# The second half of the adaLN modulation product: VectorE weighing replaced by TensorE products with the vector c

## The chip, the cores and the metric
The kernel runs on one core of one Trainium2 chip, as one launch. The metric is device time in microseconds, median of repeated executions; one further execution was profiled.

## What is computed
Two transformer-like blocks of two layers each run one after the other on 512 tokens of width 1024. Only a piece of the first block matters here: each of its layers derives six vectors of 1024 from the conditioning vector c and scales and shifts its two norms and gates its two residuals with them.

```python
c_act = jax.nn.silu(c)
for l in range(DEPTH):                                    # DEPTH = 2, D = 1024
    mod = (c_act @ ada_w[l] + ada_b[l])[:, None, :]       # ada_w[l]: 1024 x 6144, 24 MB
    sh1, sc1, g1, sh2, sc2, g2 = jnp.split(mod, 6, axis=-1)
    h = rmsnorm(x, norm_mix_g[l]) * (1.0 + sc1) + sh1
    ...                                                   # four mixers -> mix
    x = x + g1 * (mix @ w_out[l])                         # the output projection
    h = rmsnorm(x, norm_ffn_g[l]) * (1.0 + sc2) + sh2     # needs columns 3072.. of mod
    f = (silu(h @ ffn_w1[l]) * (h @ ffn_w3[l])) @ ffn_w2[l]
    x = x + g2 * f
```

## The kernel before
All large products are made in three TensorE products each (`three`, lines 1967 to 1969): weights and activations are both split into a high and a low part. ScalarE makes the high part of a weight block (L781), GpSimd the low one (L1236), and TensorE multiplies them with 512 tokens as the moving operand. A unit (`pe_unit`) is 256 output columns of a weight matrix with 1024 rows: two tiles m = 0, 1, each of 8 rows blocks k times three matmuls, into PSUM banks 0 and 1, so 48 matmuls in a unit. Weights come in units through two buffers `raw[0]`, `raw[1]`, all DMAs being issued by SyncE (SP) in program order.

The modulation matrix of a layer is cut into chunks of 256 columns (`G`). Chunks 0 to 15 (the first 4096 columns) are made elsewhere and belong to `a_raw` and `a_acc`. The last eight, `B_CHUNKS = 8`, are the ones this change touches; they are made during the output projection of the same layer:
- SP (`sp_modulation_b`, L607 to L614) loads chunk n into `b_raw[n % 2]`, a tile of 128 partitions x 8 row blocks x 256 columns. From the third chunk on it waits until chunk n - 2 has been weighed. In `sp_layer1` chunks 0 and 1 go ahead of weight unit 12, chunks 2 and 3 ahead of unit 13, and chunks 4 to 7 behind unit 13 and ahead of the first FFN weights.
- VectorE (`weigh_b`, L1674, by `dve_weigh`, L1424) multiplies row block 0 by c (L1428) and adds the seven others, each times its own c (L1431), into `b_acc`: eight instructions of 128 x 256 for each chunk. Each waits for the one before. Two chunks stand ahead of the projection's residual updates, the others are placed between them: in the loop over the eight tiles k, for k from 1 to 6, chunk k + 1 is weighed first, and then tile k of the projection is taken out of its bank (L1684, `x = bank * g1 + x`), which also frees the bank for TensorE. Sums of squares for the next norm (L1468) follow from tile 2 on.
- TensorE sums `b_acc` over its 128 partitions with a moving operand of one column, a column of ones (L2245), two output columns of bank 6 for a chunk. After each of the four projection units (`pe_layer1`, the loop over j) it does so for two chunks. The last of them lets VectorE add the bias and make the gains (L1449, L1458), which the norm ahead of the FFN needs.

After the last of these TensorE makes the sum over partitions for the norm (`pe_rms`, L2034), ScalarE takes its inverse root (L796, L798), VectorE multiplies (L1485), ScalarE makes the normed high part (L802) and the full one, VectorE the low one (L1481), and the FFN starts with the first pair of units (`pe_first_pair`). ScalarE splits FFN unit 14 ahead of its square of tile 6 and unit 15 after its square of tile 7. In this span the order on every engine is that of the program text; no scheduler moves anything.

Of the kernel before, what the change touches and what calls it, by code (L numbers as in the profile page):

```python
# [20 lines left out]
F32 = mybir.dt.float32  # L21
# [6 lines left out]
P = 128  # L28
T = 512
D = 1024  # L30
KD = D // P
NB = T // P
G = 256
# [15 lines left out]
A_CHUNKS, B_CHUNKS = 16, 8  # L49
# [61 lines left out]
def build(nc, a, table_at, out):  # L111

    with ExitStack() as ctx:
        top = [nc.sbuf_base + 31 & ~31]

        def place(name, shape, dt, at=None):

            size = 4
            for x in shape[1:]:
                size *= x  # L120
            off = top[0] if at is None else at
            t = nc.alloc_sbuf_tensor_at(name, shape, dt, offset=off)
            if at is None:
                top[0] = off + (size + 31 & ~31)
            return t

        b = Named()
# [75 lines left out]
        m = Region("m_", mid)  # L203
# [14 lines left out]
        fq_at = m.at  # L218
# [16 lines left out]
        b.rows2 = place("rows2", [2 * TAPS, P], F32, at=(nc.sbuf_usable_end & ~31) - 4 * P)  # L235

        b.b_raw = [place(f"b_raw{i}", [P, KD, G], F32, at=full_at + 4 * KD * G * i) for i in range(2)]
        b.b_acc = place("b_acc", [P, B_CHUNKS * G], F32, at=fq_at)

        n = Region("n_", mid)  # L240
        b.n_sq = n("sq", [P, KD, T])
# [43 lines left out]
        bank = [ctx.enter_context(nc.psum_tensor(f"bank{i}", [P, T], F32)) for i in range(8)]  # L285
        s = Sems(nc, ctx)
# [35 lines left out]
class Sems:  # L322

    def __init__(self, nc, ctx):
        def up(name, per, credit=0):

            return Signal(ctx.enter_context(nc.semaphore(name)), per, credit)
# [16 lines left out]
        self.par = up("par", 2)  # L344
        self.a_acc = up("a_acc", KD * A_CHUNKS, 2 * KD)
        self.a_pe = up("a_pe", 2)
        self.b_acc = up("b_acc", KD * B_CHUNKS)
        self.b_pe = up("b_pe", 1)
        self.mod = up("mod", 3)
        self.gain = up("gain", 2)  # L350
        self.a_in = [up(f"a_in{i}", 16 * A_CHUNKS // 2) for i in range(4)]
# [255 lines left out]
def sp_modulation_b(sp, e, l, n):  # L607

    s = e.s
    if n >= 2:  # L610
        sp.wait_ge(*s.b_acc(l, KD * (n - 1)))
    c = (A_CHUNKS + n) * G
    sp.dma_start(e.b.b_raw[n % 2][:, :, :], e.a["ada_w"][l, :, c:c + G].rearrange("(k p) c -> p k c", p=P))\
      .then_inc(s.b_in[n % 2].up, 16)  # L614
# [35 lines left out]
def sp_layer1(sp, e, l, more):  # L650
    a, b, s = e.a, e.b, e.s
    lay = Layer(s, 1, l)

    for j in range(2):
        sp_weights(sp, e, lay, j, a["w_in"], l, IN1[UNIT_COLS1[j]])
    sp.wait_ge(*lay.bank_free(0, 0))
    sp.wait_ge(*lay.bank_free(1, 0))
    sp.wait_ge(*s.r(l * 2, 1))
    sp.dma_start(b.decay[:, :, :], a["decay"]).then_inc(s.decay_in.up, 16)
    for m in range(2):  # L660
        sp.dma_start(b.pw[:, m, :], a["pool_w"][l, 2 * m:2 * m + 2, :, :].rearrange("e c d -> (e c) d"))\
          .then_inc(s.decay_in.up, 16)
    for j in range(2, 10):
        sp_weights(sp, e, lay, j, a["w_in"], l, IN1[UNIT_COLS1[j]])
    for j in range(4):
        if j == 2:
            sp.wait_ge(*s.gn_o(l, 2))
        if j >= 2:
            for n in (2 * j - 4, 2 * j - 3):
                sp_modulation_b(sp, e, l, n)  # L670
        sp_weights(sp, e, lay, 10 + j, a["w_out"], l, G * j)
    for n in range(4, B_CHUNKS):
        sp_modulation_b(sp, e, l, n)
    sp_ffn(sp, e, lay, 14, a["ffn_w1"], a["ffn_w3"], 0, a["ffn_w2"], l, more)
    if more:
        sp_parameters(sp, e, l + 1)
# [747 lines left out]
def dve_weigh(dve, raw, acc, c, up, base, ks=range(KD)):  # L1424

    for k in ks:
        if k == 0:
            dve.tensor_scalar(acc, raw[:, 0, :], c[:, 0:1], None, ALU.mult).then_inc(up, 1)  # L1428
        else:
            dve.wait_ge(up, base + k)  # L1430
            dve.scalar_tensor_tensor(acc, raw[:, k - ks[0], :], c[:, k:k + 1], acc, ALU.mult, ALU.add)\  # L1431
               .then_inc(up, 1)
# [20 lines left out]
def dve_gains(dve, e, l, norm):  # L1453

    s, b = e.s, e.b
    dve_mod(dve, e, l, 2 * norm)
    dve.wait_ge(*s.mod(l, 2 * norm + 1))
    dve.scalar_tensor_tensor(b.gain[:, 8 * norm:8 * norm + 8], b.mod[:, 8 + 24 * norm:16 + 24 * norm], 1.0,  # L1458
                             b.par[:, 8 * norm:8 * norm + 8], ALU.add, ALU.mult).then_inc(s.gain.up, 1)


def dve_rms_sum(dve, e, c, k, total, square):

    s = e.s
    dve.wait_ge(*s.sq(c, k + 1))
    if k > 1:
        dve.wait_ge(*s.ssq(c, k - 1))
    dve.tensor_tensor(total, total, square, ALU.add).then_inc(s.ssq.up, 1)  # L1468
# [66 lines left out]
def dve_layer1(dve, e, l, more):  # L1535
    s, b, bank = e.s, e.b, e.bank
# [134 lines left out]
    for m in range(2):  # L1671
        dve.tensor_tensor(b.ln_d[:, m, :], b.ln_d[:, m, :], b.r[:, :], ALU.mult).then_inc(s.cn_xr.up, 1)

    def weigh_b(n):  # L1674
        dve.wait_ge(*s.b_in[n % 2](l, 16 * (n // 2) + 16))
        dve_weigh(dve, b.b_raw[n % 2], b.b_acc[:, n * G:(n + 1) * G], b.c, *s.b_acc(l, KD * n))

    weigh_b(0)
    weigh_b(1)
    for k in range(KD):  # L1680
        if k >= 1 and k + 1 < B_CHUNKS:
            weigh_b(k + 1)
        dve.wait_ge(*s.tile(lay.pair(5 + k // 4), k // 2 % 2, k % 2))
        dve.scalar_tensor_tensor(b.x[:, k, :], bank[k % 2][:, :], b.mod[:, 16 + k:17 + k], b.x[:, k, :],  # L1684
                                 ALU.mult, ALU.add).then_inc(s.bank[k % 2].up, 1)
        if k >= 2:
            dve_rms_sum(dve, e, l * 2 + 1, k - 1, b.sq[:, 0, :], b.sq[:, k - 1, :])
    dve_rms_sum(dve, e, l * 2 + 1, KD - 1, b.sq[:, 0, :], b.sq[:, KD - 1, :])
    dve.wait_ge(*s.b_pe(l, 1))
    dve_gains(dve, e, l, 1)  # L1690
    dve_rms(dve, e, l * 2 + 1, b.hf, s.hl)
    dve_ffn(dve, e, lay, 14, (Q_FFN,))
# [236 lines left out]
def dve_program(dve, e):  # L1929
    s, b, bank = e.s, e.b, e.bank  # L1930
    for x in (s.bank0, s.bank1, s.up0, s.up1, s.a_acc, s.lx):
        dve.sem_inc(x.up, x.credit)
    dve_setup(dve, e)

    dve.wait_ge(s.z_x.up, KD + 2)
    with dve.Fori(0, A_CHUNKS // 4) as i:
        for p in range(2):
            dve_modulation(dve, e, 0, i, p)
    dve.wait_ge(s.z_copied.up, Z_COPIES)
    dve.wait_ge(s.trig_in.up, 16)  # L1940
    dve_trig(dve, e, 0)
    with dve.Fori(A_CHUNKS // 4, A_CHUNKS // 2) as i:
        for p in range(2):
            dve_modulation(dve, e, 0, i, p)
    for l in range(DEPTH):
        dve_layer1(dve, e, l, l < DEPTH - 1)
    dve_rms(dve, e, 2 * DEPTH, b.x, s.lhl)
    dve.wait_ge(s.trig_in.up, 32)
    dve_trig(dve, e, 1)
    for l in range(DEPTH):  # L1950
        dve_layer2(dve, e, l)
    dve_output(dve, e)
# [19 lines left out]
def pe_unit(pe, e, lay, j, q, order=range(KD), ready=None, banks=None, tokens=False):  # L1972

    pe_unit_at(pe, e, lay, j // 2, j % 2, q, order, ready, banks, tokens)
# [56 lines left out]
def pe_rms(pe, e, c, total):  # L2031
    s, b = e.s, e.b
    pe.wait_ge(*s.ssq(c, 7))
    pe.matmul(e.bank[7][:, :], b.ones[:, :], total, start=True, stop=True).then_inc(s.rms.up, 1)  # L2034
# [65 lines left out]
def pe_layer1(pe, e, l):  # L2100
    s, b, bank = e.s, e.b, e.bank
# [82 lines left out]
    for k in range(KD):  # L2184
        pe.wait_ge(*s.hf(c, k + 1))
        op = pe.matmul(bank[4][0:4, :], b.wff[:, k, :], b.hf[:, k, :], start=(k == 0), stop=(k == KD - 1))
# [31 lines left out]
    for m in range(2):  # L2218
        lone_wait(pe, s, *lay.bank_free(m, Q_POOL))
        for h in range(2):  # L2220
            o = HD * h
            op = pe.matmul(bank[m][o:o + HD, :], b.pw[o:o + HD, m, :], b.wb[o:o + HD, m, 0:T], start=True, stop=True)
# [6 lines left out]
    for m in range(2):  # L2229
        op = pe.matmul(bank[0][:, :], b.ones[:, :], b.cv[:, m, :], start=(m == 0), stop=(m == 1))  # L2230
# [3 lines left out]
    for m in range(2):  # L2234
        pe.wait_ge(*s.cn_sq(l, m + 1))
        op = pe.matmul(bank[1][:, :], b.ones[:, :], b.ln_s[:, m, :], start=(m == 0), stop=(m == 1))
    op.then_inc(s.cn_ps.up, 1)
    values(3)
    for j in range(4):
        pe_unit(pe, e, lay, 10 + j, Q_OUT + j, order=MIX_ORDER, ready=(lambda n: s.ml(l, n + 1)) if j == 0 else None)  # L2240

        pe.wait_ge(*s.b_acc(l, KD * (2 * j + 2)))
        for n in range(4 * j, 4 * j + 4):
            at = 2 * A_CHUNKS + n
            op = pe.matmul(bank[6][:, at:at + 1], b.b_acc[:, n * P:(n + 1) * P], b.ones[:, 0:1], start=True, stop=True)  # L2245
    op.then_inc(s.b_pe.up, 1)
    pe_rms(pe, e, c + 1, b.sq[:, 0, :])
    pe_ffn(pe, e, lay, 14, c + 1)

# [313 lines left out]
```

## Time and profile before

| | |
|---|---|
| median of 3 runs | 2858.13 us (2850.03 to 2858.3) |
| profiled execution | 2860.76 us, of which the span is 2858.9 us |
| mean granted TensorE clock in the span | 0.937 of full speed |
| TensorE matmul busy | 2610.1 us, 91% |
| VectorE busy | 1081.4 us, 38% |
| ScalarE busy | 876.8 us, 31% |
| GpSimd busy | 1109.1 us, 39% |
| DMA, mean | 94 GB/s |

A share of busy time is an average over the whole span. The change concerns two stretches of it, one in each layer of the first block, some 69 us long each; so the page's averages say who bounds the kernel as a whole, and a timeline of these stretches says who bounds there. A matmul's duration in the timeline holds its way through the array and overlaps the next one's: the cost of one in a row of many is the distance from start to start.

### The profile page before, as it was taken

The numbers are of one execution on the slowest core, as the hardware profiler recorded it, in microseconds if no ns is written. First come the engines' busy times: TensorE is split into PE (matmuls) and PEld (weight loads), VectorE is DVE, ScalarE is ACT, GpSimd is POOL, SyncE is SP. The second block draws the span as 40 slices with busy tenths as digits, with TensorE's granted clock in tenths as the row PEclk, the third lists the DMA queues.
The fourth block names the chain that finished last, engine by engine and source line by source line (L and its number), as shares of the span: only waits on it lengthen the run. The fifth ranks groups of instructions, "written<-read, shape, count | busy, mean of one in ns | idle before, by whom it ended". The sixth has DMA issues, their size and how long they took to land.

```text
span 2858.9 us, 30619 instructions
## 1 busy us (share of the span) xinstructions
PE 2610.1 (91%) x11550; PEld 2040.0 (71%) x11550; DVE 1081.4 (38%) x1830; ACT 876.8 (31%) x1158; POOL 1109.1 (39%) x376
## 2 busy tenths in 40 slices
PE   1599789999999779999899989999989898999998
PEld 1485568878876468887677668887868566888786
DVE  7575640018756560000159543000025954300002
ACT  1323342222323342222142452222133245322212
POOL 0232235544333225554334224555432422555441
PEclk6699889999899889999999899999999889999998
DMA  7420333247521333322232022332342111232231
GB/s 234 137 82 24 125 111 103 88 121 224 171 74 45 104 105 101 103 89 81 80 91 74 23 74 80 97 103 76 89 112 59 60 37 59 88 103 89 84 91 60
DMA packets 313580, 267.98 MB, mean 94 GB/s; under 512 B 20376, under 2 KB 306696, under 8 KB 313240
## 3 DMA queue, kind: packets, MB, share of 16 engines
q1 hardware_dynamic: 313496, 266.86, 30.1%
q8 instruction: 52, 0.85, 0.1%
q14 instruction: 32, 0.26, 0.0%
HBM read 264.74 MB, written 2.10 MB: 93 GB/s over the span
## 4 chain that ended last, share of the span: by engine, by line
PE 79%; DVE 9%; issue 6%; ACT 3%; POOL 2%; DMA 1%; DVEq 0%; SPq 0%; ACTq 0%; POOLq 0%
PE bank L1967 23%; PE bank L1969 23%; PE bank L1968 23%; DVE a_acc L1431 2%; PE bank L2257 1%; POOL w_lo L1236 1%; PE bank L2059 1%; DVE m_sq L1468 1%; DVE n_work L1809 1%; DVE n_top L1805 1%; PE bank L2170 1%; PE bank L2322 1%; PE bank L2139 1%; PE bank L2109 1%; ACT w_hi L781 1%
## 5 line engine op out<-in xcount | busy, mean ns | idle before, releaser
L1236 POOL TENSOR_TENSOR w_lo<-raw,w_hi 128x2048 fp32r<-128x2048 f32 (+1 forms) x216 | 912.1, 4223 | 1254.2 <-ACT w_hi L781 1223.4
L1967 PE MATMUL bank<-h_hi,w_lo 128*128 128x512 f32 (+1 forms) x2256 | 898.5, 398 | 52.9 <-DVE h_lo L1481 18.2
L1968 PE MATMUL bank<-h_lo,w_hi 128*128 128x512 f32 (+1 forms) x2256 | 888.3, 394 | 0.0
L1969 PE MATMUL bank<-h_hi,w_hi 128*128 128x512 f32 (+1 forms) x2256 | 887.0, 393 | 0.0
L1967 PEld LDWEIGHTS bank<-h_hi,w_lo 128*128 128x128 f32 (+1 forms) x2256 | 429.2, 190 | 166.1 <-issue 52.4
L781 ACT ACTIVATE w_hi<-raw 128x2048 fp32r<-128x2048 f32 (+1 forms) x216 | 378.0, 1750 | 505.7 <-PE bank L1969 443.5
L1968 PEld LDWEIGHTS bank<-h_lo,w_hi 128*128 128x128 f32 (+1 forms) x2256 | 429.5, 190 | 91.5 <-issue 2.4
L1969 PEld LDWEIGHTS bank<-h_hi,w_hi 128*128 128x128 f32 (+1 forms) x2256 | 429.1, 190 | 92.1 <-issue 0.4
L1528 DVE TENSOR_TENSOR f_full<-f_act,bank 128x512 f32<-128x512 f32 x88 | 60.5, 687 | 884.2 <-PE bank L1969 884.2
L1967 PE MATMUL bank<-f_hi,w_lo 128*128 128x512 f32 x704 | 280.8, 399 | 13.3 <-POOL f_lo L1248 13.3
L1969 PE MATMUL bank<-f_hi,w_hi 128*128 128x512 f32 x704 | 280.5, 398 | 0.0
L1968 PE MATMUL bank<-f_lo,w_hi 128*128 128x512 f32 x704 | 279.9, 398 | 0.0
L1248 POOL TENSOR_TENSOR f_lo<-f_full,f_hi 128x512 f32 (+1 forms) x88 | 113.9, 1295 | 185.3 <-ACT f_hi L824 185.3
L824 ACT ACTIVATE f_hi<-f_full 128x512 f32 (+1 forms) x88 | 55.6, 632 | 377.7 <-DVE f_full L1528 377.7
L1967 PEld LDWEIGHTS bank<-f_hi,w_lo 128*128 128x128 f32 x704 | 134.2, 191 | 46.4 <-issue 14.9
L1968 PEld LDWEIGHTS bank<-f_lo,w_hi 128*128 128x128 f32 x704 | 134.4, 191 | 31.3
L1969 PEld LDWEIGHTS bank<-f_hi,w_hi 128*128 128x128 f32 x704 | 133.9, 190 | 31.5
L1431 DVE SCALAR_TENSOR_TENSOR a_acc<-a_raw,c,a_acc 128x256 f32 (+1 forms) x224 | 146.0, 652 | 9.5 <-DMA a_raw<-in_ada_w 0.4
L818 ACT ACTIVATE f_act<-bank 128x512 f32<-128x512 f32 x88 | 52.9, 601 | 307.7 <-PE bank L1969 307.7
L1924 DVE TENSOR_TENSOR x<-bank,x 128x512 f32<-128x512 f32 x16 | 11.1, 692 | 235.7 <-PE bank L1969 235.7
L1580 DVE SCALAR_TENSOR_TENSOR m_cv<-m_ch,taps,m_cv 128x512 f32<-128x512 f32 x120 | 95.5, 865 | 0.1
L1967 PE MATMUL bank<-w_hi,h_lo 128*128 128x256 f32 (+1 forms) x320 | 90.8, 284 | 0.0
(290 smaller groups left out, 2403.7 us busy)
## 6 DMA issues: line engine op xcount, KB each, us to landing
raw<-in_ffn_w SPq DMA_DIRECT2D x44, 1024.0 KB
raw<-in_w_ffn_in SPq DMA_DIRECT2D x44, 1024.0 KB
raw<-in_w_in SPq DMA_DIRECT2D x34, 1024.0 KB
a_raw<-in_ada_w SPq DMA_DIRECT2D x64, 512.0 KB, 4.8
raw<-in_ffn_w SPq DMA_DIRECT2D x32, 704.0 KB
raw<-in_w_ffn_out SPq DMA_DIRECT2D x32, 704.0 KB
b_raw<-in_ada_w SPq DMA_DIRECT2D x16, 1024.0 KB, 5.0
raw<-in_w_out SPq DMA_DIRECT2D x8, 1024.0 KB
```

The source lines that it names most:

```text
L781: act.activation(b.w_hi[p][:, 0:n], b.raw[p][:, 0:n], ACT.Copy).then_inc(s.hi.up, 1)
L818: act.activation(b.f_act[:, m, :], bank[m][:, :], ACT.Silu).then_inc(s.bank[m].up, 1)
L824: act.activation(cols(b.f_hi, i * 2 + m), b.f_full[:, m, :], ACT.Copy).then_inc(s.fh.up, 1)
L1236: pool.tensor_tensor(b.w_lo[p][:, 0:n], b.raw[p][:, 0:n], b.w_hi[p][:, 0:n].bitcast(F32), ALU.subtract)\
L1248: pool.tensor_tensor(cols(b.f_lo, i * 2 + m), b.f_full[:, m, :], cols(b.f_hi, i * 2 + m).bitcast(F32), ALU.subtract).then_inc(s.fl.up, 1)
L1431: dve.scalar_tensor_tensor(acc, raw[:, k - ks[0], :], c[:, k:k + 1], acc, ALU.mult, ALU.add)\
L1468: dve.tensor_tensor(total, total, square, ALU.add).then_inc(s.ssq.up, 1)
L1528: dve.tensor_tensor(b.f_full[:, m, :], b.f_act[:, m, :], bank[2 + m][:, :], ALU.mult)\
L1580: dve.scalar_tensor_tensor(b.cv[:, m, :], b.ch[:, m, t:t + T], b.taps[:, n:n + 1], b.cv[:, m, :], ALU.mult, ALU.add).then_inc(s.conv.up, 1)
L1967: pe.matmul(out, wlo, xhi, start=start, stop=False)
L1968: pe.matmul(out, whi, xlo, start=False, stop=False)
L1969: return pe.matmul(out, whi, xhi, start=False, stop=stop)
```

## The change
VectorE no longer weighs the last eight chunks, and `b_acc` is gone. TensorE multiplies the raw chunk by c itself: the 128 x 128 block (k, m) of `b_raw` is the stationary operand, column k of `c` the moving one, and eight such products accumulate in one column of bank 6. A chunk takes 2 x 8 of them instead of two. They stand where the sums over partitions stood, two chunks after each of the four units. The semaphore `b_acc` goes too: SP now waits for TensorE to have finished chunk n - 2 before it loads chunk n, and TensorE waits for a chunk's DMA.

```diff
 def sp_modulation_b(sp, e, l, n):
     if n >= 2:
-        sp.wait_ge(*s.b_acc(l, KD * (n - 1)))
+        sp.wait_ge(*s.b_pe(l, n - 1))
...
-    def weigh_b(n):
-        dve.wait_ge(*s.b_in[n % 2](l, 16 * (n // 2) + 16))
-        dve_weigh(dve, b.b_raw[n % 2], b.b_acc[:, n * G:(n + 1) * G], b.c, *s.b_acc(l, KD * n))
-
-    weigh_b(0)
-    weigh_b(1)
     for k in range(KD):
-        if k >= 1 and k + 1 < B_CHUNKS:
-            weigh_b(k + 1)
...
-    dve.wait_ge(*s.b_pe(l, 1))
+    dve.wait_ge(*s.b_pe(l, B_CHUNKS))
...
     for j in range(4):
         pe_unit(pe, e, lay, 10 + j, Q_OUT + j, ...)
-        pe.wait_ge(*s.b_acc(l, KD * (2 * j + 2)))
-        for n in range(4 * j, 4 * j + 4):
-            at = 2 * A_CHUNKS + n
-            op = pe.matmul(bank[6][:, at:at + 1], b.b_acc[:, n * P:(n + 1) * P], b.ones[:, 0:1], start=True, stop=True)
-    op.then_inc(s.b_pe.up, 1)
+        for n in (2 * j, 2 * j + 1):
+            pe.wait_ge(*s.b_in[n % 2](l, 16 * (n // 2) + 16))
+            for m in range(2):
+                at = 2 * (A_CHUNKS + n) + m
+                for k in range(KD):
+                    op = pe.matmul(bank[6][:, at:at + 1], b.b_raw[n % 2][:, k, m * P:(m + 1) * P], b.c[:, k:k + 1],
+                                   start=(k == 0), stop=(k == KD - 1))
+            op.then_inc(s.b_pe.up, 1)
```

## Rows read from the trace of the kernel before
**Rows 1.** The page, chain that ended last: shares of the span by engine.
```profile
PE 79%; DVE 9%; issue 6%; ACT 3%; POOL 2%; DMA 1%; DVEq 0%; SPq 0%; ACTq 0%; POOLq 0%
```
**Rows 2.** Groups of instructions by line and form: count | busy us, mean ns | idle before.
```profile
L1431 DVE SCALAR_TENSOR_TENSOR b_acc<-b_raw,c,b_acc 128x256 f32<-128x256 f32 x112 | 68.4, 611 | 4.0
L2245 PE MATMUL bank<-ones,b_acc 128*128 128x1 f32 x64 | 7.6, 240 | 0.0
```
**Rows 3.** Windows over both layers: length, busy us (count) by engine, clock, DMA.
```profile
316.50:385.50 69.00, 52.90 (x228) 41.46 (x226) 54.20 (x85) 22.13 (x26) 22.68 (x7) 0.89 0.49 159
975.30:1044.30 69.00, 52.88 (x227) 41.48 (x226) 57.88 (x85) 22.25 (x26) 22.54 (x7) 0.89 0.49 158
```
**Rows 4.** Timeline of TensorE, layer 0: start us, us, engine, line, operation, [idle before].
```profile
331.13 0.95 PE L2245 MATMUL bank<-ones,b_acc 128*128 128x1 f32 x8
331.95 0.47 PE L1967 MATMUL bank<-h_hi,w_lo 128*128 128x512 f32 x1
...
342.96 0.95 PE L2245 MATMUL bank<-ones,b_acc 128*128 128x1 f32 x8
...
355.00 0.79 PE L1967 MATMUL bank<-h_hi,w_lo 128*128 128x512 f32 x1 [5.50 <-DVE x L1684]
...
376.94 2.08 PE L2034 MATMUL bank<-m_sq,ones 128*128 128x512 f32 x2 [1.45 <-DVE m_sq L1468]
385.57 0.76 PE L1967 MATMUL bank<-h_hi,w_lo 128*128 128x512 f32 x1 [6.56 <-DVE h_lo L1481]
```
**Rows 5.** Timeline of VectorE in the same stretch.
```profile
346.21 4.17 DVE L1468 TENSOR_TENSOR m_sq<-m_sq 128x512 f32<-128x512 f32 x1 [5.19 <-ACT m_sq L789]
...
350.68 3.61 DVE L1431 SCALAR_TENSOR_TENSOR b_acc<-b_raw,c,b_acc 128x256 f32<-128x256 f32 x7
354.20 0.74 DVE L1684 SCALAR_TENSOR_TENSOR x<-bank,mod,x 128x512 f32<-128x512 f32 x1
...
374.74 0.75 DVE L1684 SCALAR_TENSOR_TENSOR x<-bank,mod,x 128x512 f32<-128x512 f32 x1 [3.69 <-PE bank L1969]
...
380.43 3.85 DVE L1485 TENSOR_TENSOR m_sq<-x,r 128x512 f32<-128x512 f32 x3 [3.27 <-ACT r L798]
```
**Rows 6.** Timeline of TensorE at other places: long batches of one-column products.
```profile
52.94 6.96 PE L2109 MATMUL bank<-ones,a_acc 128*128 128x1 f32 x32 [33.50 <-DVE a_acc L1431]
...
104.74 6.83 PE L2109 MATMUL bank<-ones,a_acc 128*128 128x1 f32 x32
...
756.51 4.57 PE L2109 MATMUL bank<-ones,a_acc 128*128 128x1 f32 x32
```
**Rows 7.** Windows over the last of these batches, L2109 on TensorE alone: length, busy (count), clock, DMA.
```profile
757.50:758.50 1.00, 1.00 (x11) 1.00 0.00 0
759.00:760.00 1.00, 1.00 (x7) 0.50 0.00 0
```
**Rows 8.** Timeline of TensorE after the batch at 104.74.
```profile
111.43 0.77 PE L1967 MATMUL bank<-h_hi,w_lo 128*128 128x512 f32 x1
112.00 0.63 PE L1968 MATMUL bank<-h_lo,w_hi 128*128 128x512 f32 x1
...
117.12 0.46 PE L1968 MATMUL bank<-h_lo,w_hi 128*128 128x512 f32 x1
```
**Rows 9.** Windows, all engines, layer 0: columns as in rows 3.
```profile
355.00:360.00 5.00, 5.00 (x13) 3.94 (x14) 4.75 (x10) 0.61 (x1) 0.00 (x0) 0.54 0.64 210
...
389.00:391.00 2.00, 2.00 (x7) 1.56 (x7) 1.89 (x4) 2.00 (x4) 0.00 (x0) 0.67 0.00 0
```
**Rows 10.** Timeline of the DMA queue, ScalarE and GpSimd, layer 0.
```profile
331.26 28.59 SPq L613 DMA_DIRECT2D b_raw<-in_ada_w  x4
360.28 58.15 SPq L587 DMA_DIRECT2D raw<-in_ffn_w  x6
...
368.65 1.92 ACT L781 ACTIVATE w_hi<-raw 128x2048 fp32r<-128x2048 f32 x1 [2.70 <-DMA raw<-in_ffn_w]
...
378.03 4.50 POOL L1236 TENSOR_TENSOR w_lo<-raw,w_hi 128x2048 fp32r<-128x2048 f32 x1 [2.53 <-ACT w_hi L781]
```

More of the change, by code:

```diff
@@ L237, in build @@
         b.b_raw = [place(f"b_raw{i}", [P, KD, G], F32, at=full_at + 4 * KD * G * i) for i in range(2)]
-        b.b_acc = place("b_acc", [P, B_CHUNKS * G], F32, at=fq_at)
         n = Region("n_", mid)
@@ L346, in __init__ @@
         self.a_pe = up("a_pe", 2)
-        self.b_acc = up("b_acc", KD * B_CHUNKS)
-        self.b_pe = up("b_pe", 1)
+        self.b_pe = up("b_pe", B_CHUNKS)
         self.mod = up("mod", 3)
```

## The prediction, on record before the changed kernel was run
> **What bounds the kernel now.** I read the page's chain first: TensorE holds 79% of it, VectorE 9% [rows 1]. So TensorE's own time counts nearly everywhere, and VectorE only where TensorE waits for it. Then the groups: VectorE's weighing of the last eight chunks is 68.4 us (and 5.5 us for the first row blocks), TensorE's part of the same work 7.6 us [rows 2]. On the page's averages TensorE, busy for 91%, is the wrong engine to give work to and VectorE, at 38%, the wrong one to relieve; but the stretch decides. In the two stretches concerned VectorE is busy for 54.20 and 57.88 of 69 us and TensorE for 52.9 [rows 3]: here they are rivals, and the weighing is three quarters of VectorE's time. The two layers look alike, so I work out one and double it.
>
> The stretch that changes runs from the end of the first projection unit (331.13) to the first FFN matmul (385.57): 54.44 us [rows 4]. Three units of 48 matmuls take 11.0 us each where nothing stops them (331.95 to 342.96), so 33.0 us. The rest is 21.4 us: four batches of eight one-column records, 0.82 us from their start to the next unit's (331.13 to 331.95), 3.3 us; a stall of 5.50 us at 355.00, with a slow restart; 1.45 us ahead of the norm's sum; and 8.63 us from that sum (376.94) to the FFN [rows 4]. The stall is the weighing's: a sum of squares of 4.17 us, seven weighing steps of 3.61 us and only then the residual update at 354.20 that frees the bank [rows 5]. It also costs clock: with TensorE idle the granted clock fell to 1.2 GHz, and over 355 to 360 it averages 0.54 [rows 9].
>
> **What goes.** Eight chunks of weighing a layer, 37 us of VectorE. Of it only the stall was on TensorE's path: 5.5 us, and with it the half-speed restart (about 4.6 us at 0.43 instead of 0.23 us a matmul, some 2.1 us lost). The 4 x 0.82 us go as well, since the new batches replace them. Nothing else is late next: the residual update behind tile 3 still waits for the slow sum of squares ahead of it, but in the meantime TensorE has a batch of at least 7 us to do. The other sum of squares, mod and gains follow the last tile by about 2 us, under the last batch.
>
> **What comes.** 8 chunks x 2 halves x 8 row blocks = 128 products in a layer, 32 in a batch. The trace has 64 matmul records of L2245 for 32 products of the program [rows 2]: an fp32 product is two load-and-multiply pairs. So a batch is 64 pairs. The price of a pair is that of L2109, the same shape, a 128 x 128 fp32 block against one column: 32 pairs took 6.96 and 6.83 us, 0.214 us a pair, at 1.2 GHz [rows 6], and 11 pairs in each 1 us but the edges, 0.111 us a pair, at 2.4 GHz [rows 7]. The latter is what a batch costs if the clock stays up: 64 x 0.1115 = 7.1 us. The two passes of one product already add into the same column there, so I add nothing for adding up.
>
> **The clock decides between these prices.** The batch at 756.51 began behind dense work at 2.4 GHz, ran without a gap, and yet the clock fell within it, 2.0 to 2.5 us after its start; the window from 759 holds 7 records at 0.50 [rows 6, 7]. And the batches at 52.94 and 104.74, nearly 7 us each of back-to-back pairs, stayed at half speed from end to end [rows 6]. 512-column matmuls behind the latter began at 111.43 and ran 0.427 us apart (12 steps from 112.00 to 117.12), until the clock rose 5.7 us after their start [rows 8]. So one-column products, however tightly packed, neither hold the clock nor bring it back. The present batches of 0.82 us are too short to show it. The Trainium skill, "TensorE: Matmul & The Clock Gate", section "Loop structure matters more than you think", promises that back-to-back matmuls stay warm; taken at its word the batches would cost 7.1 us each. The trace disagrees (0.214 us a pair behind a fall to 0.50), and that rule is the first rival below.
>
> How far into a batch it falls is not tied to the batch's start: 2.0 to 2.5 us in the only case. For the stall it is about 3 us (TensorE idle from 349.5, windows at 0.54 behind it), and between rise and fall the chip takes its own moments: rises come 5.7 us after dense work starts [rows 8], about 4.5 us behind 355.00 and behind 385.57 [rows 4, 9]. I take 3.5 us (bounds 2 and 5). A batch is then 3.5 + (64 - 31.4) x 0.2137 = 10.5 us (bounds 11.8 and 9.1). A unit behind it starts at half speed for 5 us (4.5 to 5.7), losing 5 x (1 - 0.2275 / 0.4267) = 2.3 us: 13.3 us (13.1 to 13.7).
>
> **Queues and waits.** SP now waits for TensorE before chunks 2 to 7, with weight unit 13 behind chunk 3 and the FFN weights behind chunk 7. Chunk 7's load waits for chunk 5, the end of the third batch, then the first FFN weights go out. They took 368.65 - 360.28 = 8.4 us to land, 1.9 us on ScalarE, and some 4.6 us on GpSimd [rows 10]; the second copy waits on ScalarE for the square of the last tile. That puts the second low part some 8 us behind the last unit's end, while the FFN can't start for over 17 us after it. A chunk is asked for when the one two before it is done, so a unit (11 us) and half a batch or more before its own turn, above the 8.4 us of that row. All hidden; if the cover went, the second copy would cost what it is late. One gain: VectorE's three multiplications at 380.43 took 3.85 us where the usual one takes 0.68; the first waited for GpSimd's second copy (378.03 + 4.50) [rows 5, 10]. After, that copy is done in time: 1.8 us less, 8.63 - 1.8 = 6.8 us from the norm's sum to the FFN. The last batch stands ahead of the norm's sum on TensorE, so it is exposed in full.
>
> **The sum for a layer**, from 331.13: four batches 4 x 10.5 = 41.9; three units 3 x 13.3 = 39.9; the tail 6.8; together 88.6 us against 54.4: +34 us. Bounds: late falls and early rises, 4 x 9.1 + 3 x 13.1 + 6.8 = 82.5, +28.1; the reverse, and the tail as it is, 4 x 11.8 + 3 x 13.7 + 8.6 = 96.9, +42.5. Two layers: +68 us (56 to 85). The profiled execution would go from 2860.76 to 2929; it lies 2.6 us above the median, so the median of 2858.13 goes to **2926 us**.
>
> **Rivals.**
> 1. The clock holds through the batches (weight loads count as work for the gate). Batches 7.1, units 11.0: 28.5 + 33.0 + 6.8 = 68.3, +13.9 a layer, 2886 us. For it: the engine never idles. Against: rows 6 and 7. 0.07.
> 2. It gets faster. Freed are 21.4 - 6.8 = 14.6 us a layer, so it is faster if the four batches together cost less than that, 256 pairs at under 0.057 us, with the clock up. The place would be the load of the next block hiding entirely under the product before it, or one pass instead of two: 128 pairs x 0.1115 = 14.3 us, 0.3 us a layer better, 2857.5 us; with both, 128 x 0.057 = 7.3 us, 7.3 us a layer better, 2843.5 us. For it: nothing but VectorE's being the crowded engine here. Against: two records for each product, 0.1115 us for each. Faster 0.02; within 0.3%, by one of the two, 0.02.
> 3. The 16 passes into one PSUM column do not overlap: each waits out the product before, 0.24 us by the record's mean duration [rows 2] instead of the distance. Batches 15.4 at either clock: 61.4 + 39.9 + 6.8 = 108.1, +53.7 a layer, 2965 us. For it: sixteen in a row aren't in the trace, only two. Against: pairs of one product and of two products lie equally far apart. 0.06.
> 4. The change does less than it says (the batches wait for data, the queue of SP binds): every wait that I found is covered by 5 us or more; a wait of 5 us in one batch would give 10 us more, and lies inside the range. Not kept apart.
>
> **Chances.** Forecast 0.83, the rivals 0.07, 0.04, 0.06. 0.3% of 2858 is 8.6 us, about what a measurement of this kernel can tell from no change. Slower holds the forecast and rivals 1 and 3: 0.96. The range is the forecast's own bounds, 2914 to 2943, widened on the low side towards rival 1 and slightly above for a wait: 2906 to 2945.
>
> **What would show it.** No VectorE instruction of L1428 or L1431 between the projection's residual updates, and no stall of TensorE for L1684. Four batches of 64 matmul records between the units, 9 to 12 us each, about 0.11 us apart at first and 0.21 later; the clock down within each batch and up 4 to 6 us into the next unit; the FFN's first matmul some 88 us behind the first batch's start; the mean clock of the span down from 0.937 to about 0.926 (some 35 us a layer more at half speed: (2859 x 0.937 + 68 - 35) / 2927). The forecast is wrong if the batches keep 2.4 GHz (+28 us remain), if pairs in an accumulating row lie further apart than 0.214 us, or if the first FFN matmul waits for GpSimd's copy.

## The result

The changed kernel takes 2916.16 us in the median (2914.71 to 2919.93), the kernel before 2855.6 us beside it. The ratio is 1.0212, with a 95% interval of 1.0196 to 1.0227: 2.1% slower, some 60 us. The forecast was 2926 us, +68, within 2906 to 2945. The profiled execution took 2917.59 us, its span is 2915.8.

The page of the changed kernel: VectorE is relieved by 78 us, TensorE busy for 73 us more, and the new products have a line of their own in the chain (L2237 in the last line). The second line answers to [rows 1]: TensorE 81% instead of 79%, VectorE 8% instead of 9%.

```profile
PE 2683.5 (92%) x11998; PEld 2113.7 (72%) x11998; DVE 1003.2 (34%) x1702; ACT 876.7 (30%) x1158; POOL 1108.1 (38%) x376
...
PE 81%; DVE 8%; issue 6%; ACT 3%; POOL 2%; DMA 1%; DVEq 0%; SPq 0%; ACTq 0%; POOLq 0%
PE bank L1957 23%; PE bank L1958 23%; PE bank L1959 23%; PE bank L2237 2%; DVE a_acc L1429 2%; PE bank L2250 1%; POOL w_lo L1234 1%; PE bank L2049 1%; DVE n_work L1799 1%; DVE n_top L1795 1%; PE bank L2160 1%; PE bank L2315 1%; PE bank L2129 1%; PE bank L2099 1%; PE bank L2348 0%
```

Its groups by form hold 512 records for the 256 products, two each; this answers to [rows 2].

```profile
L2237 PE MATMUL bank<-c,b_raw 128*128 128x1 f32 x512 | 78.6, 290 | 0.0
```

The timeline of TensorE in layer 0, the answer to [rows 4]. Each line of L2237 is one batch of 64 pairs, the next line the first matmul of the unit behind it.

```profile
329.38 9.65 PE L2237 MATMUL bank<-c,b_raw 128*128 128x1 f32 x64
338.89 0.77 PE L1957 MATMUL bank<-h_hi,w_lo 128*128 128x512 f32 x1
...
352.27 8.73 PE L2237 MATMUL bank<-c,b_raw 128*128 128x1 f32 x64
360.87 0.77 PE L1957 MATMUL bank<-h_hi,w_lo 128*128 128x512 f32 x1
...
373.58 9.49 PE L2237 MATMUL bank<-c,b_raw 128*128 128x1 f32 x64
382.94 0.77 PE L1957 MATMUL bank<-h_hi,w_lo 128*128 128x512 f32 x1
...
396.48 11.69 PE L2237 MATMUL bank<-c,b_raw 128*128 128x1 f32 x64
408.04 2.06 PE L2024 MATMUL bank<-m_sq,ones 128*128 128x512 f32 x2
414.70 0.77 PE L1957 MATMUL bank<-h_hi,w_lo 128*128 128x512 f32 x1 [4.61 <-DVE h_lo L1479]
```

From the first batch to the FFN it takes 414.70 - 329.38 = 85.3 us where it took 54.4. From start to start the batches take 9.5, 8.6, 9.4 and 11.6 us, the units between them 13.4, 12.7 and 13.5, the tail 6.7. TensorE never waits between 329.38 and the end of the norm's sum: the 5.50 us stall of [rows 4] is gone. The windows tell where the length comes from (columns as in [rows 3]: the granted clock is the number behind the busy figures of the five engines):

```profile
329.40:338.90 9.50, 9.50 (x66) 9.50 (x64) 0.75 (x1) 1.91 (x1) 4.52 (x1) 0.73 0.34 110
338.90:343.90 5.00, 5.00 (x13) 3.94 (x14) 0.00 (x0) 0.00 (x0) 0.00 (x0) 0.50 0.75 244
344.00:352.00 8.00, 8.00 (x36) 6.63 (x36) 0.75 (x1) 0.00 (x0) 0.00 (x0) 1.00 0.32 107
352.30:360.90 8.60, 8.60 (x66) 8.60 (x64) 5.33 (x3) 4.09 (x5) 4.52 (x1) 0.81 0.37 122
373.60:382.90 9.30, 9.30 (x65) 9.30 (x64) 1.35 (x2) 0.63 (x1) 0.00 (x0) 0.74 0.37 115
396.50:408.00 11.50, 11.50 (x65) 11.50 (x64) 2.37 (x3) 2.43 (x2) 5.82 (x2) 0.59 0.46 147
...
1018.40:1027.40 9.00, 9.00 (x66) 9.00 (x64) 0.75 (x1) 1.91 (x1) 4.52 (x1) 0.77 0.35 117
1041.30:1052.50 11.20, 11.20 (x65) 11.20 (x64) 5.33 (x3) 4.10 (x5) 4.52 (x1) 0.61 0.28 94
1065.80:1074.50 8.70, 8.70 (x65) 8.70 (x64) 1.35 (x2) 0.63 (x1) 0.00 (x0) 0.80 0.37 121
1087.10:1096.60 9.50, 9.50 (x66) 9.50 (x64) 3.26 (x3) 2.43 (x2) 6.74 (x2) 0.73 0.39 117
```

All eight batches begin at 2.4 GHz and end at 1.2. Since the clock is at one of these two levels, a mean of 0.73 over 9.5 us means (0.73 - 0.5) / 0.5 = 46% of it at the upper one, 4.4 us; in the order of the lines 4.4, 5.3, 4.5, 2.1, 4.9, 2.5, 5.2 and 4.4 us, 4.2 in the mean. The unit behind starts at 0.50 (second line, 13 matmuls in 5 us) and is at 1.00 from 344 on (36 in 8 us).

The stretch from the first batch to the FFN grows by 30.9 us in layer 0 and by 30.4 in layer 1 (989.87 to 1044.33 before, 1018.36 to 1103.25 now), 61.3 us together. The FFN starts 29.1 us later in layer 0 (385.57 to 414.70), 58.9 us later in layer 1 (1044.33 to 1103.25), and the span ends 56.9 us later, so the rest of the kernel is 4 us shorter in this execution than in the one before.

### The profile page after: what moved, and what is told of

Same layout as the page of the kernel before. It is cut to its first block, busy times and chain, and to the rows that moved or that the text cites. A ratio compares the mean times of both kernels' runs of the same rounds, so it can differ in the third digit from the quotient of the medians.

```text
span 2915.8 us, 31387 instructions
## 1 busy us (share of the span) xinstructions
PE 2683.5 (92%) x11998; PEld 2113.7 (72%) x11998; DVE 1003.2 (34%) x1702; ACT 876.7 (30%) x1158; POOL 1108.1 (38%) x376
## 4 chain that ended last, share of the span: by engine, by line
PE 81%; DVE 8%; issue 6%; ACT 3%; POOL 2%; DMA 1%; DVEq 0%; SPq 0%; ACTq 0%; POOLq 0%
PE bank L1957 23%; PE bank L1958 23%; PE bank L1959 23%; PE bank L2237 2%; DVE a_acc L1429 2%; PE bank L2250 1%; POOL w_lo L1234 1%; PE bank L2049 1%; DVE n_work L1799 1%; DVE n_top L1795 1%; PE bank L2160 1%; PE bank L2315 1%; PE bank L2129 1%; PE bank L2099 1%; PE bank L2348 0%
## 5 line engine op out<-in xcount | busy, mean ns | idle before, releaser
L1957 PE MATMUL bank<-f_hi,w_lo 128*128 128x512 f32 x704 | 280.8, 399 | 13.3 <-POOL f_lo L1246 13.3
```

The costliest lines, as they stand in the source:

```text
L1957: pe.matmul(out, wlo, xhi, start=start, stop=False)
```

## The experiments

All kernels ran beside the kernel before. The question: how much of the 60 us is the pairs themselves, how much the clock, and what relieving VectorE gave back.

**1. The relief alone.** Based on the changed kernel; seven of eight row blocks are left out (and `start` and `stop` are True for the one that stays), so that TensorE has as many small products as before:

```diff
-                for k in range(KD):
+                for k in range(1):
```

> The changed kernel with only row block 0 of each chunk multiplied: 4 products (8 pairs) a batch as before, 7 of 8 row blocks of the second half of the modulation are left out. It shows what the relief of VectorE is worth by itself. My theory: the 5.50 us stall ahead of unit 2 goes for the most part (some 1.5 us stays, since the bank of tile 3 still waits for a sum of squares that waits for ScalarE), its half-speed restart goes (2.1 us), GpSimd's second copy may still delay the norm: 6 to 9 us a layer less than before, 2840 to 2846 us. The difference to the changed kernel, about 75 us, is then what 4 x 56 further pairs a layer cost with the clock that they lose, not the relief. Rival: VectorE was never in the way, this kernel takes as long as before (within 3 us), and the 60 us are the whole price of the batches.

Measured: 2858.73 us, ratio 1.0000 (0.9988 to 1.0013). The rival's number came out. But most of the stall did go, as the theory said; the time was lost again at the end of the stretch, in a place whose price I had not worked out. TensorE, VectorE and GpSimd of this kernel in layer 0:

```profile
350.63 0.50 PE L1957 MATMUL bank<-h_hi,w_lo 128*128 128x512 f32 x1 [1.59 <-DVE x L1674]
...
368.03 0.95 PE L2237 MATMUL bank<-c,b_raw 128*128 128x1 f32 x8
379.76 2.08 PE L2024 MATMUL bank<-m_sq,ones 128*128 128x512 f32 x2 [10.77 <-DVE m_sq L1466]
...
370.22 9.48 DVE L1466 TENSOR_TENSOR m_sq<-m_sq 128x512 f32<-128x512 f32 x2 [1.23 <-ACT m_sq L787]
...
369.74 9.41 POOL L1234 TENSOR_TENSOR w_lo<-raw,w_hi 128x2048 fp32r<-128x2048 f32 x2 [20.38 <-ACT w_hi L779]
```

The stall ahead of tile 5 is 1.59 instead of 5.50 us, and the last small batch comes at 368.03 instead of 374.54. The norm's sum, though, waits 10.77 us instead of 1.45 [rows 4] (10.39 in layer 1). VectorE's last two sums of squares take 9.48 us, where two took 1.48 elsewhere, since GpSimd's two splits of the first FFN weights run beside them without a break. The Trainium skill, "SBUF — State Buffer", section "SBUF: two separate sides", says that a VectorE operation with two SBUF inputs and a GpSimd operation that reads SBUF take a shared port pair as an exclusive lock, so that the one that comes second waits. The trace agrees: the two sums end at 379.70, 0.55 us behind the second split's end (379.15), and the single one at 345.74 ends 0.55 us behind the split of 344.74, too (4.17 us instead of 0.68). The splits come that late because the weights land at 367.76 only (issued at 358.17, behind the chunks' DMAs), and ScalarE makes its square of tile 6 behind the high part of the first of them.

**2. The same with the FFN weights earlier.** On SP's queue, the first two FFN units go ahead of chunks 6 and 7:

```diff
-    for n in range(4, B_CHUNKS):
+    for n in (4, 5):
         sp_modulation_b(sp, e, l, n)
-    sp_ffn(sp, e, lay, 14, a["ffn_w1"], a["ffn_w3"], 0, a["ffn_w2"], l, more)
+    for p, w in enumerate((a["ffn_w1"], a["ffn_w3"])):
+        sp_unit(sp, e, lay, 7, p, w8(b.raw[p]), w[l, :, 0:G].rearrange("(k p) c -> p k c", p=P))
+    for n in (6, 7):
+        sp_modulation_b(sp, e, l, n)
+    sp_ffn(sp, e, lay, 14, a["ffn_w1"], a["ffn_w3"], 0, a["ffn_w2"], l, more, first=1)
```

`first=1` lets its loop over the FFN's unit pairs start at the second.

> e1_relief (7 of 8 row blocks of the second half of the modulation left out, VectorE relieved) with the same early FFN weights. Theory: relieving VectorE by itself gives 6 us a layer once the splits are out of the way: the norm's sum 2 us behind the last batch instead of 11, 2845 us against e1_relief's 2859. Rival: no gain in the end, as e1_relief.

Measured: 2844.8 us, ratio 0.9955 (0.9939 to 0.9971), as the theory had it. GpSimd's splits now lie at 358.59 and 370.40, the two last sums between them, and the norm's sum 1.45 us behind the batch:

```profile
367.78 1.48 DVE L1470 TENSOR_TENSOR m_sq<-m_sq 128x512 f32<-128x512 f32 x2
...
358.59 4.61 POOL L1238 TENSOR_TENSOR w_lo<-raw,w_hi 128x2048 fp32r<-128x2048 f32 x1 [10.37 <-ACT w_hi L783]
370.40 4.50 POOL L1238 TENSOR_TENSOR w_lo<-raw,w_hi 128x2048 fp32r<-128x2048 f32 x1 [7.21 <-ACT w_hi L783]
...
369.31 1.12 PE L2028 MATMUL bank<-m_sq,ones 128*128 128x512 f32 x2 [1.45 <-DVE m_sq L1470]
```

In the trace the stretch from the first batch to the FFN takes 48.4 and 48.8 us in the two layers, against 54.4 and 54.5. So taking the weighing off VectorE is worth 13 us in both layers together, if the splits are out of the way, and nothing if they aren't. The same early weights in the kernel before:

> The kernel before with only the early FFN weights, VectorE's order as it was. Theory: GpSimd's first split comes some 2 us earlier only (it stands behind the square of tile 5 on ScalarE), the second stays where it is behind the square of the last tile, the stall stays: same as before within 3 us, so that e5's gain is of both steps together. Rival: the late weights alone are what binds, 8 us less than before.

Measured: 2855.09 us, ratio 0.9984 (0.9968 to 0.9999): some 4 us, at the edge of what shows, where I had expected no more than 3. They are not in this stretch: in the trace it takes 54.9 us in each layer, 0.4 more than before, and the stall is 5.50 us as before. Early weights alone are not the 13 us; it takes both.

**3. The clock, by a wider moving operand.** Based on the changed kernel; c's column is read 128 times over by a stride of 0:

```diff
-   op = pe.matmul(bank[6][:, at:at + 1], b.b_raw[n % 2][:, k, m * P:(m + 1) * P], b.c[:, k:k + 1],
+   op = pe.matmul(bank[6][:, at:at + P], b.b_raw[n % 2][:, k, m * P:(m + 1) * P], b.c[:, k:k + 1].to_broadcast([P, P]),
```

> The changed kernel with the moving operand of each product widened from 1 to 128 columns (c's column repeated by a stride of 0; the columns behind the wanted one are overwritten or unused), the result is the same. More work on TensorE: 128 columns in fp32 should take a quarter of the 0.53 us that 512 take, 0.134 us a pair at 2.4 GHz instead of 0.111. Theory (the gate looks at what streams, not at whether instructions are packed): the clock holds in the batches, 8.6 us each, units 11.0, 4 x 8.6 + 3 x 11.0 + 6.8 = 74 us from the first batch to the FFN instead of 85.3: 11 us a layer faster than the changed kernel although it streams 128 times the columns, about 2894 us. Rival (the gate falls for another reason: fp32 passes, load-bound pairs, bank 6): it falls as now, batches 13 to 14 us, about 2948 us.

Measured: 2877.82 us, ratio 1.0068 (1.0050 to 1.0085). By the medians 38 us less than the changed kernel, with 128 times the columns. TensorE's timeline and, below it, a window over the whole stretch:

```profile
330.69 7.31 PE L2237 MATMUL bank<-c,b_raw 128*128 128x128 f32 x64
...
384.93 7.31 PE L2237 MATMUL bank<-c,b_raw 128*128 128x128 f32 x64
...
330.70:392.00 61.30, 61.30 (x401) 55.54 (x399) 17.65 (x14) 12.14 (x12) 16.78 (x4) 1.00 0.50 162
```

The clock stays at 2.4 GHz up to the end of the last batch, in both layers, and each batch ahead of a unit takes 7.06 us to the unit's first matmul. I had expected 8.6, but a pair costs at most 0.1115 us, as with one column. That the columns stream while the next block loads would explain it; no row here shows it.

This is the cleanest pair of kernels of the study: same instructions, same data read, same order, and only the moving operand differs. The stretch from the first batch to the FFN takes 69.3 and 69.4 us instead of 85.3 and 84.9, 31.4 us less. It still holds waits of 2.06 and 2.15 us for VectorE's last sums, which the slower batches had covered. With these taken out, the fallen clock costs some 36 us in the changed kernel.

Another candidate for the fall was the DMA of the next chunk, which starts in the middle of a batch. In seven of the eight batches it is running within the microsecond in which the clock falls; in the eighth there is none (windows of TensorE alone: clock, DMA share, GB/s). And in the kernel above the same loads run beside the batches at a clock of 1.00.

```profile
333.40:334.40 1.00, 1.00 (x8) 0.69 0.28 62
...
1043.30:1044.30 1.00, 1.00 (x9) 0.72 0.00 0
```

**4. The clock, by the place of the products.** Two products behind each of the 16 three-matmul steps of a unit (`between`, chunk 2j + m in the half m), instead of 32 behind the unit:

```diff
+                if between is not None and n < KD - 1:
+                    between(m, n)
         op.then_inc(s.half.up, 1)
+        if between is not None:
+            between(m, KD - 1)
...
-        for n in (2 * j, 2 * j + 1):
...
```

> The changed kernel's products, all of them, but two behind each of the 16 three-matmul steps of their own unit instead of 32 behind the unit. Same instructions, same count. Theory (half of the loss is the clock that falls in a stretch of one-column products): with dense work in between, the clock holds; a unit takes 11.0 + 7.1 = 18.1 us, unit 0 takes part of it in its waits for GpSimd, no batch stands behind the last unit: some 13 us a layer over before, about 2883 us, 33 us faster than the changed kernel; this is also what the pairs cost at 2.4 GHz alone. Rival (pairs cost what they cost wherever they are; the fall comes anyhow): as the changed kernel, 2916, or slower, since a clock that fell once could not rise within a diluted unit: up to 2990.

Measured: 2879.93 us, ratio 1.0090 (1.0060 to 1.0119), 36 us less than the changed kernel, against 33 expected. The units run at full clock with the one-column products among them (first window; 0.99 over 989 to 1064 in layer 1); four pairs and three 512-column matmuls take 1.14 us, so a pair takes 0.114 us. The windows ahead of the norm's sum and across it (columns as before):

```profile
316.50:389.50 73.00, 73.00 (x450) 64.48 (x447) 11.71 (x13) 15.96 (x18) 17.54 (x6) 1.00 0.42 137
389.50:400.50 11.00, 1.59 (x6) 0.71 (x6) 8.09 (x10) 6.39 (x8) 4.50 (x1) 0.70 0.30 95
```

The second window holds what this order gives up: with no batch behind the last unit the norm's sum waits 1.90 us, and the FFN comes 8.63 us behind it, as before the change, instead of 6.66. That is 3.9 us a layer which the changed kernel doesn't have; on the other side the products of the first unit fill some of its waits for GpSimd. So the 36 us are near the clock's part, but are not that part alone.

**5. Shorter batches.** Row blocks 0 to 3 only (`for k in range(4)`, the other half of the products is left out), 32 pairs a batch:

> The changed kernel with row blocks 0 to 3 of 8 only (half of the products of the second half of the modulation are left out): batches of 32 pairs, 3.6 us at 2.4 GHz. Theory: the clock falls when a batch is long enough, and a batch of 32 pairs is near that: it falls in some batches and not in others, so they are 3.6 us where it holds and 4.5 to 5.5 us with a slow unit behind them where it falls; the price is less than half of the full batches': 2858 + 10 to 25 us. Rival: the clock falls in every batch as it does with 64 pairs and the units behind start slow: 2858 + 30 us or more, half of the price and more.

Measured: 2867.98 us, ratio 1.0038 (1.0023 to 1.0053), +11 us for half of the pairs where all of them cost +60. In layer 0:

```profile
329.47 3.63 PE L2237 MATMUL bank<-c,b_raw 128*128 128x1 f32 x32
...
345.58 4.75 PE L2237 MATMUL bank<-c,b_raw 128*128 128x1 f32 x32
...
363.29 3.63 PE L2237 MATMUL bank<-c,b_raw 128*128 128x1 f32 x32
...
377.80 3.63 PE L2237 MATMUL bank<-c,b_raw 128*128 128x1 f32 x32
```

The clock fell within one of the eight batches (the second of layer 0; 4.61 us to the unit behind it, the others 3.49), and soon behind two others, within the unit (12.6 us instead of 11.0 for the units behind the first of layer 0 and the second of layer 1). By the medians twice the pairs cost five times as much; by the two stretches of the traces, 65.9 and 63.1 us here, 20 us in sum against 61, it is three times. Not all of that is the clock: the last batch here lies ahead of a wait for VectorE's sums (7.28 us left, 10.77 in e1_relief), which it only shortens.

**6. Clock and queue mended together.** Wide operand and early weights:

> e2_wide (128-column moving operand, right result) with the same early FFN weights. In e2_wide the last sums of squares took 8.45 us beside GpSimd's back-to-back splits and put the norm's sum 2.3 us behind the last batch. Theory: these 2.3 us go in each layer, about 2873 us, still 15 us over before: with clock and queue mended, the change costs what its pairs cost at 2.4 GHz less the relief. Rival: same as e2_wide, 2878.

Measured: 2880.45 us, ratio 1.0083 (1.0063 to 1.0104); no gain over e2_wide, the rival's number. The profile shows that the theory's step did happen: the norm's sum comes at the end of the last batch (391.74), and the stretch takes 67.0 us in both layers where e2_wide has 69.3 and 69.4. These 2.3 us a layer are too little beside what executions of these kernels differ by (2870 to 2889 for e2_wide, 2877 to 2884 here). For the sum it matters that this kernel and e6_relief_early differ only in the products: 1.0083 - 0.9955 = 0.0128 of 2858 us, 37 us for the pairs at full clock.

**7. The relief without TensorE.** Can VectorE keep the weighing and the stall still go? On the kernel before:

> The kernel before, with VectorE keeping the weighing, but in another order: chunks 0 and 1 are weighed ahead of the wait for ScalarE's inverse root of the convolution's norm (VectorE is idle there for 10.8 us), each tile's residual update goes ahead of the next chunk's weighing, and the first sum of squares is put behind tile 3. Nothing is added to TensorE. Theory: the 5.50 us stall was one of order, not of VectorE's load; it goes, with its 2.1 us of restart: 7 to 8 us a layer, about 2842 us, which is all that relieving VectorE could give, at no cost on TensorE. Rival: VectorE is really full in this stretch (54 of 69 us), the stall moves to another tile or to the norm's sum, and the time stays within 3 us of before.

Measured: 2861.75 us, ratio 1.0020 (1.0007 to 1.0033), slower by 4 to 6 us, a miss. As in e1_relief the stall shrinks and the stretch gives it back. In layer 0 it is the same meeting of splits and sums of squares (9.42 and 9.13 us, and the norm's sum waits 9.10). In layer 1 the split comes earlier and holds up the weighing of the last chunk instead, 7.78 us for seven steps that take 3.61 elsewhere, and TensorE's small sum waits 3.48 us for it. With the early weights:

> e4_order, with the DMAs of the first two FFN weight units put ahead of those of chunks 6 and 7 on SP's queue. In the trace of e4_order the stall of 5.50 us ahead of unit 2 is down to 1.3 us, but the norm's sum comes 9.4 us behind the last batch instead of 1.7: the FFN weights land at 368.6, their two splits on GpSimd run back to back (9.42 us) right when VectorE wants its last two sums of squares (9.13 us for two instead of 1.4). Theory: the relief is real and is given back there, since the first split comes too late and meets the end of the projection; with the weights loaded earlier the first split is over before the last tile, the norm's sum comes 2 to 3 us behind the last batch, the FFN some 4 us a layer earlier than before: about 2850 us, the first version below the kernel before. Rival: the end of the stretch is bound by something else (the second split, behind the square of the last tile): within 3 us of before.

Measured: 2854.76 us, ratio 0.9989 (0.9979 to 1.0000); 3 us instead of 8, no better than the early weights alone; the stretch takes 54.3 us in each layer. What remained were TensorE's small sums waiting for chunks that were weighed late (1.87, 0.94 and 2.49 us in layer 0). So the chunks were moved further ahead:

```diff
+    weigh_b(2)
+    weigh_b(3)
     for k in range(KD):
...
-        if k >= 1 and k + 1 < B_CHUNKS:
-            weigh_b(k + 1)
+        if k in (1, 2, 4, 5):
+            weigh_b({1: 4, 2: 5, 4: 6, 5: 7}[k])
```

(the residual update of tile k stands first, in place of the line of dots; chunks 0 and 1 stand ahead of the wait for the convolution's norm and the first sum of squares behind tile 3, as in the two kernels before it, and chunk 6's DMA between those of the two FFN units).

> VectorE keeps the weighing; chunks 0 to 3 are weighed ahead of the first residual update (0 and 1 in the wait for the convolution's norm, 2 and 3 while TensorE is in unit 0), 4 and 5 behind the updates of tiles 1 and 2, 6 and 7 behind those of tiles 4 and 5; the updates always go first; the first FFN weights go ahead of the DMAs of chunks 6 and 7. In e5's trace what is left in this stretch are waits of TensorE's small sums for chunks 2 and 3 (2.25 us behind unit 1), 4 and 5 (1.3 us) and 6 and 7 (2.9 us within unit 3). Theory: with the chunks earlier these go too, units run back to back from unit 0 to the norm's sum, 8 us a layer less than before: 2843 to 2847 us, as e6_relief_early, which left most of the weighing out. Then all that the change could gain is to be had without TensorE. Rival: GpSimd's splits and VectorE's weighing stand in each other's way wherever they are put (a weighing step beside a split took 4.4 us more), and the time is e5's, 2855.

Measured: 2841.86 us, ratio 0.9941 (0.9920 to 0.9963), 0.6% below the kernel before and the fastest that gives the whole result, with VectorE doing all of its work. TensorE in layer 0:

```profile
329.91 0.95 PE L2253 MATMUL bank<-ones,b_acc 128*128 128x1 f32 x8
341.74 0.95 PE L2253 MATMUL bank<-ones,b_acc 128*128 128x1 f32 x8
353.57 0.95 PE L2253 MATMUL bank<-ones,b_acc 128*128 128x1 f32 x8
366.14 1.05 PE L2253 MATMUL bank<-ones,b_acc 128*128 128x1 f32 x8 [0.59 <-DVE b_acc L1434]
370.06 2.08 PE L2042 MATMUL bank<-m_sq,ones 128*128 128x512 f32 x2 [2.86 <-DVE m_sq L1471]
378.69 0.76 PE L1975 MATMUL bank<-h_hi,w_lo 128*128 128x512 f32 x1 [6.56 <-DVE h_lo L1484]
```

The first three small sums are 11.8 us apart, the fourth comes after 12.6, with a wait of 0.59; 378.69 - 329.91 = 48.8 us instead of 54.4 (47.6 in layer 1).

## Why the prediction was right, and where it was not

**The sum.** By ratios to the kernel before: relief -0.0045 (e6_relief_early), pairs at full clock +0.0128 (e7_wide_early against it), fallen clock 1.0212 - 1.0083 = +0.0129; together +0.0212. In us of 2858: -13, +37, +37. The parts are steps from one measured kernel to the next and so add up by construction, but the traces give the same by themselves. The two stretches together take 108.9 us before, 97.2 in e6_relief_early, 134.0 in e7_wide_early and 170.2 in the changed kernel: -12, +37, +36. The clock's part was forecast at 2 x (13.4 us of batches + 6.9 us of units) = 41 us. The 37 us for the pairs are net: at 7.06 instead of 0.82 us the four batches add 25 us a layer, and some 6 of these lie in waits that e6_relief_early still has.

The steps, one by one:

- **Two pairs for each product, at 0.1115 and 0.214 us**: right. 512 records; e2_wide's batches show 64 pairs in 7.06 us. Rival 3, passes that don't overlap when they add up in one column, is refuted by that and by the changed kernel's batches, 8.6 to 11.6 us where it has 15.4.
- **The clock falls within each batch and rises only in the next unit**: right in eight of eight. Rival 1 is out: its 2886 us is its forecast of the kernel with a clock that holds, and the kernels in which it held, e2_wide and e3_spread, are 8 and 6 us from it. The Trainium skill, "TensorE: Matmul & The Clock Gate", section "Loop structure matters more than you think", promises that back-to-back matmuls stay warm; for these one-column products the trace disagrees, with a granted clock of 0.50 at the end of eight of eight batches.
- **How far into the batch**: mis-sized. I took 3.5 us, 4.2 were measured (2.1 to 5.3, as wide as my bounds of 2 to 5). Batches of 10.5 us were forecast, 9.7 measured in the mean of eight (77.5 us in sum). That is 83.8 - 77.5 = 6.3 us, nearly all of the 7 us by which the two stretches came out below the forecast (68.4 forecast, 61.3 measured). The only batch in the trace before fell 2.0 to 2.5 us after its start, and six of the eight here took 4.4 to 5.3.
- **Units behind a batch**: 13.3 us forecast, 13.2 measured in six.
- **The tail**: 6.8 us forecast, 6.66 measured. The three multiplications that had taken 3.85 us beside GpSimd's split [rows 5] take 1.90 us, since that split is over by then.
- **Layers**: 85.3 and 84.9 us from batch to FFN against 88.6 forecast and 54.4 before. In layer 0 the stretch also began 1.75 us earlier (329.38 instead of 331.13). 0.4 us of it is GpSimd's low parts, 3.75 instead of 4.11 us with no weighing beside them; the rest was there ahead of the changed stretch and I have no cause for it but the differences between executions. In e1_relief, which has the same VectorE program, it began 0.5 us earlier only.
- **"Nothing else is late next"**: right for this kernel, wrong as a price of the relief. In the changed kernel the last sums of squares take 1.80 us and are over at 399.15, long before the last batch ends at 408.04, so it hides them. e1_relief and e4_order show that without such a batch the splits are late next, by 9.3 us (10.77 against 1.45) and, in layer 0, by 7.7 us (9.10); both of their forecasts failed on the step that carried this sentence over to them. The sum came out well here because the new work covered the spot: in this place the prediction was lucky.
- **Waits and queues**: all covered, as said. SP's FFN weights go out at 383.91, and GpSimd's second split ends at 399.98 + 4.51 = 404.5, 10 us ahead of the FFN. Rival 4 never came.
- **Rival 2**, faster below 0.057 us a pair: the pairs stayed at 0.1115 even at full clock, twice that.
- **The mean clock**: 0.926 forecast, 0.931 measured, down from 0.937.
- **A reading**: by the groups the weighing is 37 us a layer of 54 to 58, two thirds of VectorE's time in the stretch and not three quarters. Nothing in the sum rests on it.

VectorE was the crowded engine of the stretch [rows 3], and yet giving its work to TensorE was wrong: of 37 us of weighing a layer only some 6 were on the path, and e9_all_early got those back by order and early weights, without TensorE.

## What to carry to other kernels

Price work that moves to TensorE by what the trace shows of the granted clock beside such work, and not only by its duration. Here batches of 64 one-column pairs let the clock fall in eight of eight cases, and were paid for again in the dense matmuls behind them; the same products spread between dense ones, or with a moving operand of 128 columns at the same 0.1115 us a pair, did not pay it. Before an engine is relieved, ask what of its work is on the path at all: here order, and a weight load placed a few DMAs earlier, gave all that the relief could give. And a stall that is taken away is only a gain if the next meeting point is free; look at what GpSimd does there beside VectorE's sums.

## What the runs showed of the hardware

- Widening the moving operand of an fp32 product from 1 to 128 columns left the distance of the pairs at 0.1115 us, and turned the granted clock from 0.77 (329.4 to 408.0 of the changed kernel, first to last batch) to 1.00 (330.7 to 392.0 of e2_wide).
- The price of a one-column pair depended on its surroundings: 0.21 us at the end of a batch of 64 (9.4 us for the last 45 pairs of the batch at 396.48, an estimate from its fall 2.1 us after its start), 0.114 us when four of them stood between dense matmuls, though the products were as many and as narrow.
- VectorE's sums of two SBUF tensors waited out GpSimd's splits: 0.68 us alone, 4.1 to 4.2 when begun 1 us into one split, 9.48 for two beside two. Residual updates, with one operand in PSUM, took 0.75 us beside a split, too (374.74 before the change, with a split from 370.65 to 375.50).
- What remains open: the moment of the fall within a batch varied from 2.1 to 5.3 us in one execution; no run here ties it to anything in the kernel.
- Open as well: of e8_early's 4 us nothing lies in the stretch that was changed, and a median of these kernels can hold a few us that come from elsewhere.
